# Four modulation pieces to one PSUM region, score products of two heads on opposite row halves, and two steps moved

## What is computed

```python
# both layers: six modulation vectors per stream from the conditioning
def _ada(cond, w, b):
    m = (jax.nn.silu(cond) @ w + b)[:, None, :]
    return jnp.split(m, N_MOD, axis=-1)
# even layer: scores over 128 + 64 (rotary) columns of a head, 4 heads
def _mla_block(qb, k, v):
    s = jnp.einsum('bqhd,bkhd->bhqk', qb, k).astype(jnp.float32) * MLA_SCALE
    p = jax.nn.softmax(s, axis=-1).astype(v.dtype)
    return jnp.einsum('bhqk,bkhd->bqhd', p, v)
# odd layer: 6 heads, two score maps (m) of 64 columns each
def _diff_block(qb, k, v, lam, subln_g, lam_init):
    s = jnp.einsum('bqhmd,bkhmd->bhmqk', qb, k).astype(jnp.float32) * DIFF_SCALE
    p = jax.nn.softmax(s, axis=-1)
    a = (p[:, :, 0] - lam * p[:, :, 1]).astype(v.dtype)
    o = jnp.einsum('bhqk,bkhe->bqhe', a, v)
    return _rms_norm(o, subln_g) * (1.0 - lam_init)
```

## Time and profile before

| what | value |
|---|---|
| median of 3 runs | 1722.41 us (1716.16 to 1723.5) |
| profiled execution | 1721.32 us, its span 1719.8 us |
| PE busy | 1657.8 us (96%) |
| DVE, ACT busy | 1062.3 us (62%), 942.7 us (55%) |
| DMA | 426.29 MB, mean 248 GB/s |
| chain that ended last | PE 91%, DVE 3%, ACT 3%, DMA 2% |

### The profile page before, as it was taken

How to read it: one execution, slowest core, us unless ns; L and a number is a source line. 1 busy time by engine, 2 the same in 40 slices (tenths; PEclk the granted TensorE clock), 3 DMA queues, 4 the chain that set the end, 5 groups by cost and what they waited for, 6 DMA issues and landing times.

```text
span 1719.8 us, 23106 instructions
## 1 busy us (share of the span) xinstructions
PE 1657.8 (96%) x8546; PEld 1323.3 (77%) x8546; DVE 1062.3 (62%) x1380; ACT 942.7 (55%) x1372; POOL 37.8 (2%) x60
## 2 busy tenths in 40 slices
PE   6998999899999999999988999999999999999997
PEld 3785458798888888688756888888888888888885
DVE  2341331452222333454474899999999989999998
ACT  4412432462222322462365677777877777777875
POOL 0000000040000000000000100000000000000000
PEclk9998999899999999999999999999999999999999
DMA  8524374369222222272205899999999999999992
GB/s 336 199 74 196 139 255 171 115 245 375 98 98 98 98 99 98 74 254 105 74 1 196 355 421 375 396 358 396 356 412 354 400 382 377 384 367 393 364 354 75
DMA packets 67709, 426.29 MB, mean 248 GB/s; under 512 B 8624, under 2 KB 12464, under 8 KB 19760
## 3 DMA queue, kind: packets, MB, share of 16 engines
q1 hardware_dynamic: 59856, 396.93, 60.2%
q0 software_dynamic: 7776, 28.32, 4.2%
HBM read 401.62 MB, written 23.59 MB: 247 GB/s over the span
## 4 chain that ended last, share of the span: by engine, by line
PE 91%; DVE 3%; ACT 3%; DMA 2%; issue 1%; SPq 0%; ACTq 0%; DVEq 0%
PE ps L1654 26%; PE ps L1656 26%; PE ps L1655 26%; PE ps L1672 3%; PE ps L1696 2%; PE ps L1813 2%; DMA raw<-in_w 1%; PE ps L1705 1%; PE ps L2097 1%; DMA x<-in_x 1%; PE ps L1862 1%; DVE small L1207 1%; PE ps L1844 1%; PE ps L1860 1%; DVE wl L1004 1%
## 5 line engine op out<-in xcount | busy, mean ns | idle before, releaser
L1501 DVE TENSOR_TENSOR wl<-raw,wh 128x1024 fp32r<-128x1024 f32 x522 | 615.7, 1222 | 62.4 <-ACT wh L908 55.8
L908 ACT ACTIVATE wh<-raw 128x1024 fp32r<-128x1024 f32 x522 | 523.0, 1053 | 97.1 <-PE ps L1656 97.1
L1654 PE MATMUL ps<-wh,ah 128*128 128x512 f32 (+1 forms) x800 | 310.2, 388 | 0.9 <-issue 0.2
L1654 PE MATMUL ps<-ah,wh 128*128 128x512 f32 (+1 forms) x848 | 301.9, 356 | 6.0 <-DVE al L1119 3.3
L1656 PE MATMUL ps<-wh,al 128*128 128x512 f32 (+1 forms) x800 | 302.5, 378 | 0.0
L1655 PE MATMUL ps<-wl,ah 128*128 128x512 f32 (+1 forms) x800 | 302.1, 378 | 0.0
L1655 PE MATMUL ps<-al,wh 128*128 128x512 f32 (+1 forms) x848 | 294.0, 347 | 0.0
L1656 PE MATMUL ps<-ah,wl 128*128 128x512 f32 (+1 forms) x848 | 293.9, 347 | 0.0
L1004 DVE TENSOR_TENSOR wl<-raw,wh 128x1024 fp32r<-128x1024 f32 x120 | 141.5, 1222 | 142.9 <-ACT wh L485 142.9
L1654 PEld LDWEIGHTS ps<-ah,wh 128*128 128x128 f32 x848 | 161.7, 191 | 29.7 <-issue 4.3
L1655 PEld LDWEIGHTS ps<-al,wh 128*128 128x128 f32 x848 | 161.7, 191 | 20.7 <-issue 1.0
(11 more groups left out here) (251 smaller groups left out, 1582.5 us busy)
## 6 DMA issues: line engine op xcount, KB each, us to landing
raw<-in_w SPq DMA_DIRECT2D x372, 1024.0 KB, 6.3
sent<-raw POOLq DMA_DIRECT2D x16, 512.0 KB, 24.4
back<-raw POOLq DMA_DIRECT2D x16, 512.0 KB, 25.1
x<-sent POOLq DMA_DIRECT2D x7, 512.0 KB, 12.2
back<-x POOLq DMA_DIRECT2D x7, 512.0 KB, 9.0
x<-in_x SPq DMA_DIRECT2D x1, 2048.0 KB, 13.6
raw<-in_ukv SPq DMA_DIRECT2D x1, 1024.0 KB, 7.3
out<-raw SPq DMA_DIRECT2D x4, 256.0 KB, 3.4
```

The costliest lines, as they stand in the source:

```text
L908: act.activation(wh[:, J % SPLITS, piece_half(h)], slot(J % SLOTS)[:, piece_half(h)], ACT.Copy).then_inc(w_hi, 1)
L1501: ins = dve.tensor_tensor(wl[:, J % SPLITS, piece_half(h)], slot(J % SLOTS)[:, piece_half(h)], wh[:, J % SPLITS, piece_half(h)].bitcast(F3 ...
L1654: pe.matmul(out, lh, rh, start=start, stop=False)
```

## The change

Four modulation pieces n = 4q + j now add into one region (`JOINT = 4`): piece j uses a window of `condP` that is shifted by 2j columns, so that its two data rows come to rows 2j and 2j + 1. One copy `rows(q)` and one `mod_cols(q)` (8 columns wide) serve four pieces. The pieces are spread otherwise: 8 to 11 before the projections, 12 to 30 in the even attention loop, 31 to 34 after units 2 to 5 of the even output projection, the rest as before; the ring's order follows. `take_modulation` reads the new column order. In the even attention the units of two heads alternate, and PE issues two units' scores in every other turn: both 128-row products, then both rotary products. In the odd attention the queries are evacuated with the factor -1/8, so that the minimum over the scores is the bias and L1208 goes; scaling takes two operations; the first unit's scores are issued in the middle of the last input piece, and those of unit i + 1 behind the transposes of unit i - 2. `eps` and `pick_rows` move within `small`.

```diff
+JOINT = 4
...
-NORM_MODS, ATT_MODS, GAP_MODS = 16, 35, 40
+NORM_MODS, ATT_MODS, OUT_MODS, GAP_MODS = 12, 31, 35, 40
...
-            + mods(NORM_MODS, ATT_MODS) + main(M_WOUT + 3, M_GU + 2) + mods(ATT_MODS, GAP_MODS) + main(M_GU + 2, M_OIN + 2)
+            + mods(NORM_MODS, ATT_MODS) + main(M_WOUT + 3, M_GU) + mods(ATT_MODS, ATT_MODS + 2) + main(M_GU, M_GU + 1)
+            + mods(ATT_MODS + 2, OUT_MODS) + main(M_GU + 1, M_GU + 2) + mods(OUT_MODS, GAP_MODS) + main(M_GU + 2, M_OIN + 2)
...
+        condP = area(15616, 2 * (JOINT - 1) + KD * 32)
+
+        def cond_columns(k, j):
+
+            at = 2 * (JOINT - 1) + 32 * k - 2 * j
+            return condP[:, at:at + 32]
...
-            def rows(n):
-                act.wait_ge(mod_used, n + 1)
-                if n >= 2:
-                    act.wait_ge(sem("mod_cols"), n - 1)
-                act.activation(mod_row(n), ps[:, 6 + n % 2, 0:256], ACT.Copy).then_inc(sem("mod_rows"), 1)
-            rows(0)
-            rows(1)
+            def rows(q):
+                act.wait_ge(mod_used, JOINT * q + JOINT)
+                if q >= 2:
+                    act.wait_ge(sem("mod_cols"), q - 1)
+                act.activation(mod_row(q), ps[:, 6 + q % 2, 0:256], ACT.Copy).then_inc(sem("mod_rows"), 1)
...
+                    if i == 0 and begun:
+                        begun()
...
-                    if name == "mla":
-                        rows(NORM_MODS + i)
+                    if name == "mla" and (NORM_MODS + i) % JOINT == JOINT - 1:
+                        rows((NORM_MODS + i) // JOINT)
...
-                    act.activation(q_o[:, 2 * p:2 * p + 2, :], ps[:, bank:bank + 2, 0:TL], ACT.Copy).then_inc(evac_act, 1)
+                    act.activation(q_o[:, 2 * p:2 * p + 2, :], ps[:, bank:bank + 2, 0:TL], ACT.Copy, scale=-DIFF_SCALE).then_inc(evac_act, 1)
...
+            def last_piece():
+                project(OIN - 1)
+                act.wait_ge(sem("four_ps"), 2)
+                act.activation(ah[:, 6:8, 0:TL], ps[:, 6, :].rearrange("p (a b) -> p a b", a=2), ACT.Copy
+                               ).then_inc(sem("four_hi"), 1)
...
+                            src = ps[:, 2 * ((i + 1) % 2):2 * ((i + 1) % 2) + 2, :]
+                        if name == "diff":
+                            dve.tensor_reduce(small[:, cols], src, AX.X, ALU.min).then_inc(s_("negmax"), 1)
+                        else:
+                            link(dve.tensor_reduce(small[:, cols], src, AX.X, ALU.max))
+                            dve.tensor_scalar(small[:, cols], small[:, cols], -scale, None, ALU.mult).then_inc(s_("negmax"), 1)
...
-                link(dve.tensor_scalar(small[:, at + 1:at + 2], small[:, at + 1:at + 2], small[:, 7:8], None, ALU.mult))
-                link(dve.tensor_scalar(pr_o[:, i % 2, 0, :], pr_o[:, i % 2, 0, :], small[:, at:at + 1], None, ALU.mult))
-                return dve.scalar_tensor_tensor(out=pr_o[:, i % 2, 0, :], in0=pr_o[:, i % 2, 1, :],
-                                                scalar=small[:, at + 1:at + 2], in1=pr_o[:, i % 2, 0, :],
-                                                op0=ALU.mult, op1=ALU.add)
-
-            attention("diff", ounits, DIFF_SCALE, scaled_o, lambda u: None)
+                first, second = (pr_o[:, i % 2, m, :] for m in range(2))
+                link(dve.tensor_scalar(second, second, small[:, at + 1:at + 2], small[:, 7:8], ALU.mult, ALU.mult))
+                return dve.scalar_tensor_tensor(out=first, in0=first, scalar=small[:, at:at + 1], in1=second, op0=ALU.mult, op1=ALU.add)
...
+                q, j = divmod(n, JOINT)
                 pe.wait_ge(*ring_landed("mod", n))
-                if n >= 2:
-                    pe.wait_ge(sem("mod_rows"), n - 1)
+                if j == 0 and q >= 2:
+                    pe.wait_ge(sem("mod_rows"), q - 1)
                 w = slot(ring_slot("mod", n))
                 for k in range(KD):
-                    j = 32 * (k % 4)
-                    mm = pe.matmul(ps[j:j + 32, 6 + n % 2, 0:256], condP[:, k, :], w[:, k * 256:(k + 1) * 256],
-                                   start=(k < 4), stop=(k >= 4))
+                    at = 32 * (k % 4)
+                    mm = pe.matmul(ps[at:at + 32, 6 + q % 2, 0:256], cond_columns(k, j), w[:, k * 256:(k + 1) * 256],
+                                   start=(j == 0 and k < 4), stop=(j == JOINT - 1 and k >= 4))
                 mm.then_inc(mod_used, 1)
 
-            def mod_cols(n):
-                pe.wait_ge(sem("mod_rows"), n + 1)
+            def mod_cols(q):
+                pe.wait_ge(sem("mod_rows"), q + 1)
+                at = 256 + 48 * (JOINT * q // MOD_LAYER0) + 4 * JOINT * (q % (MOD_LAYER0 // JOINT) // 2)
+                out = ps[:, 6 + q % 2, at:at + 4 * JOINT].rearrange("p (j c s) -> p j c s", c=2, s=2)
                 for c in range(2):
-                    at = 256 + 48 * (n // MOD_LAYER0) + 4 * (n % MOD_LAYER0 // 2) + 2 * c
-                    mm = pe.matmul(ps[:, 6 + n % 2, at:at + 2], mod_row(n)[:, c * P:(c + 1) * P], pick_rows,
-                                   start=True, stop=True)
+                    mm = pe.matmul(out[:, :, c, :], mod_row(q)[:, c * P:(c + 1) * P], pick_rows, start=True, stop=True)
...
             def filler(n):
 
                 mod_piece(n)
-                mod_cols(n - 1)
+                if n % JOINT == 1 and n > JOINT:
+                    mod_cols(n // JOINT - 1)
 
...
+                if n == 1:
+                    mod_cols(2)
...
+                def score(i):
+                    if paired and i % 2:
+                        return
+                    if i >= 2:
+                        pe.wait_ge(s_("exp"), i if paired else i - 1)
+                    if paired:
+                        scores(i)
+                    else:
+                        scores(i).then_inc(s_("scores"), 1)
+
                 for i in range(len(units) + 3):
-                    if i < len(units):
-                        if i >= 2:
-                            pe.wait_ge(s_("exp"), i - 1)
-                        scores(i).then_inc(s_("scores"), 1)
+                    if begun <= i < (2 + ahead if ahead else len(units)):
+                        score(i)
                     filler(i)
                     if 2 <= i <= len(units) + 1:
                         u = i - 2
@@ -1834,6 +1854,8 @@
                         for b in range(units[u][2] // P):
                             mm = pe.transpose(ps[:, tb + u % 2, b * P:(b + 1) * P], pr(u, b), ident)
                         mm.then_inc(s_("turned"), 1)
+                    if ahead and 2 <= i < len(units) - ahead:
+                        score(i + ahead)
...
             def unit_filler(i):
                 mod_piece(NORM_MODS + i)
-                if i:
-                    mod_cols(NORM_MODS + i - 1)
+                if i > 1 and (NORM_MODS + i) % JOINT == 1:
+                    mod_cols((NORM_MODS + i) // JOINT - 1)
             def scores_e(i):
-                h, j, n, k0 = units[i]
-                pe.matmul(ps[:, i % 2, 0:n], q_nope[:, h, j * P:(j + 1) * P], k_nope[:, h, k0:k0 + n], start=True, stop=False)
-                r = slice(64 * (h % 2), 64 * (h % 2) + 64)
-                return pe.matmul(ps[:, i % 2, 0:n], q_pe[r, h // 2, j * P:(j + 1) * P], k_pe[r, k0:k0 + n],
-                                 start=False, stop=True)
+                for u in (i, i + 1):
+                    h, j, n, k0 = units[u]
+                    pe.matmul(ps[:, u % 2, 0:n], q_nope[:, h, j * P:(j + 1) * P], k_nope[:, h, k0:k0 + n], start=True, stop=False)
+                for u in (i, i + 1):
+                    h, j, n, k0 = units[u]
+                    r = slice(64 * (h % 2), 64 * (h % 2) + 64)
+                    pe.matmul(ps[:, u % 2, 0:n], q_pe[r, h // 2, j * P:(j + 1) * P], k_pe[r, k0:k0 + n],
+                              start=False, stop=True).then_inc(sem("mla_scores"), 1)
             attention("mla", units, scores_e,
...
+                if u == 2:
+                    pe.wait_ge(scales_ready, 2)
+                    mod_piece(ATT_MODS)
+                if 3 <= u <= 5:
+                    filler(ATT_MODS + u - 2)
...
+            def first_scores():
+                pe.wait_ge(evac_act, evacs(("i", 8), "act"))
+                pe.wait_ge(sem("orope_done"), 4)
+                scores_o(0).then_inc(sem("diff_scores"), 1)
+
...
-    return [(h, j, T if j < 2 else TL, 0 if j < 2 else TL) for h in range(HEADS) for j in range(4)]
+    return [(h, j, T if j < 2 else TL, 0 if j < 2 else TL) for g in range(HEADS // 2) for j in range(4) for h in (2 * g, 2 * g + 1)]
```

More of the change, by code:

```diff
@@ L558, in _ @@
             root(N_E1)
-            for n in range(MOD_FIRST - 2, MOD_FIRST):
-                rows(n)
+            rows(1)
             act.wait_ge(scales_ready, 1)
@@ L586, in _ @@
             root(N_KV)
[L587 to L588 removed]
+            rows(2)
             dsts = ([q_nope[:, h, :] for h in range(HEADS)] + [q_pe[:, g, :] for g in range(HEADS // 2)]
```

146 lines of the change are left out of this document (68 added, 78 removed).

## The result

| | before | changed |
|---|---|---|
| median, us | 1722.86 (1716.16 to 1723.5, 4 runs) | 1692.51 (1691.86 to 1693.49, 4 runs) |
| profiled execution, us (span) | 1721.3 (1719.8) | 1691.86 (1690.2) |

The ratio is 0.9833, 95% interval 0.9808 to 0.9858: faster by 1.7%, clear of noise. A second series of the changed kernel gave 0.9829 (0.9815 to 0.9842), median 1691.24. The forecast was 1693.

A forecast was written before the change was run, and what follows sets the result against it. PE was taken to bound the even attention, PE and DVE to be equally busy in the odd. Terms -0.5 - 16.5 - 8.9 + 2.8 - 1.4 - 4.1 = -28.6 us from 1721.3 gave 1692.7, said as 1693; range 1683 to 1704.

The forecast's parts named there:

- before and in the projections: Projections start 14.3 us earlier, high clock saves 2.7 us, one column product adds 0.46 us: -16.5 us, bounds -18 and -10.
- even attention: Even attention: column products -6.9, paired scores -7.3, new waits +5.6, last column product gone but DVE's last subtraction awaited -0.3: -8.9 us.
- even output projection: Four pieces and one column product come in, +4.5 us; after the wait for piece 37, -1.7 us: +2.8, bounds +1 and +4.5.
- odd input projection: 712 to 770.7 us: six column products go, three behind waits, so three counted: -1.4 us, bounds 0 and -2.8.
- odd attention: DVE's unit shortens from 2.97 to 2.64 us, -3.6 us; with first maximum and scores -4.1 us in all, bounds -1.5 and -6.
- The pair: Even attention scores, two heads together: 2.87 us against 4.00, 1.6 against 2.3 with 256 keys, rotary products overlapping: -7.3 us.
- A: Low clock stays in the projections or comes earlier: gain there 2.7 to 7 us less, 1698 us; chance 0.12.
- B: Even attention: row halves don't overlap inside a bank that 128-row products opened: +6.7 us, 1699 us; chance 0.06.
- F: Column sharing fails because a region must wait for its copy: at most 1 us a region, 1700 us; chance 0.02.
- C: Waits in the even attention of 10 us or more, DVE and ACT working in bursts: 1698 us; chance 0.08.
- D: Few new waits and more gain from the later stages: 1686 us; chance 0.09.
- E: Slower than before: clock falls in the even attention, +50 us at half rate, 1743 us; chance 0.03.

The follow-up runs named there:

- Experiment 4: Changed kernel with eight modulation pieces before the projections and none in the even output projection, regions still shared by four: 1700.75 us, ratio 0.9881.
- experiment 3: Unpaired: changed kernel with one unit's scores a turn, each waiting for the exponential two turns back: 1693.61 us, ratio 0.9841.
- experiments 1: Rotary products apart: changed kernel with each head's rotary product right behind its own 128-row product: 1699.95 us, ratio 0.988.
- Experiment 7: Changed kernel with the ring filled in another order, pieces 31 to 34 and then 35, 36 before the gate/up pieces that would block them: 1689.82 us, ratio 0.9822.
- Experiment 5: Changed kernel with DVE's odd-attention turn long again, one more 2-column operation and scaling in three operations: 1697.44 us, ratio 0.9885.
- experiment 6: Changed kernel with the odd attention's scores issued late as before, ACT's last piece and DVE's low part in front: 1694.33 us, ratio 0.9855.
- 9: Changed kernel with DVE's subtraction behind the scaling of the turn instead of in front of it: 1691.4 us, ratio 0.9835.
- experiment 2: Changed kernel with both rotary products of a pair on rows 0 to 63, order and waits unchanged: 1697.91 us, ratio 0.9867.

## Why the prediction was right, point by point

| step | forecast, us | measured, us |
|---|---|---|
| start | -0.5 | -1.3 |
| before and in the projections | -16.5 | -16.7 |
| even attention | -8.9 | -8.1 |
| even output projection | +2.8 | +4.0 |
| odd input projection | -1.4 | -3.9 |
| odd attention | -4.1 | -4.7 |
| rest | 0 | +1.1 |
| sum, spans | -28.6 | -29.6 |

The odd attention is counted with the +1.3 us by which the stretch in front of it grew, mostly the first scores' 1.1 us: -5.95 + 1.3. The rest is the odd output projection with the router, 56.6 and 57.5 us, and the experts. That the sums agree to 1 us is in part luck: the seven differences add up to 7.2 us without their signs.

- **Before the projections.** The projections began 14.4 us earlier counted from the first large matmul (forecast 14.3), and at the high clock: no low clock between 43.2 and 315.7 us. Experiment 4 brings both back, though it prices the whole move at 8 to 9.5 us net of the output projection where the forecast's terms make 12 (16.5 less 4.5); the part with which shared regions speed up eight pieces, 3.1 us (24.2 to 21.1), had no term of its own.
- **Even attention.** The column products were sized right (-6.9 against -6.6 of busy time, experiment 3). The pair was priced too high (-7.3 against -5.3) and the waits as well (+5.6 against +3.2); these two errors cancel to 0.3 us, which is luck. Most of the remaining error is the last term, forecast at -0.3: from before to unpaired the idle time rose by 0.5 us (0.64 to 1.18). In the pair's term the overlap is full, as the earlier trace rows had it. The Trainium skill's 3.07 times for four row tiles, 77% of the full factor (TensorE: Matmul & The Clock Gate, section on packing small matmuls), would by the prediction's estimate make 1.36 us of a rotary pair; measured are 1.05. Of the 2.0 us by which the pair's term is off, the score products are 0.3: the changes of row count were mis-sized, 0.2 us and not 0.1, so that a pair of 512 keys takes 2.97 and not 2.87 us. 0.7 us is the dearer work beside modulation pieces, for which the sum had no term, and 1.0 us are waits that the profile books as work (experiment 3). The 66.82 - 63.83 = 3.0 us of busy time between unpaired and rotary products apart, which hold the same instructions, divide in the same way: 1.3 us in the 128-row scores (a unit behind value products takes 2.0 us, one behind other scores 2.11), 1.3 in the value products, 0.4 in the rest.
- **Even output projection.** Pieces and products came to what was forecast, but "nothing in the change frees it sooner, so that wait and the dip of the clock behind it stay" missed that the ring's order also puts pieces 35 and 36 behind the second gate/up piece, which waits for the first one's split. PE's waits for transfers went from 3.3 to 5.2 us. Experiment 7 takes 3.1 of them away: -3.6 us.
- **Odd input projection.** The step that failed most, outside its own bounds: "three stand behind waits for normalised chunks, so I count three". All six column products came off PE's busy time (53.85 to 50.63 us). The waits did not grow in their place: idle time fell by 0.7 us as well, a wait of 0.9 us for a transfer among it.
- **Odd attention.** The turn is 2.58 us, not 2.64. Experiment 5 shows DVE's operations, 0.39 us a turn in ten turns. Of the early scores experiment 6 shows +1.8 us, but most of it is their place behind the transposes, which the prediction gave no term, and 0.4 us the first maximum off the path. The stage before and after had some low clock each (0.94 and 0.96), so its -4.7 us are good to about 1 us only.
- **Rivals.** A, B and F didn't occur. C and D stayed out: 4.4 us idle in the attention, between them. E didn't occur in the changed kernel (even attention at 1.00 in both profiles), but showed for a few microseconds in experiments 4 and 9. The prediction's "the transfers hold" is so in both profiles of the changed kernel, but not in those of all variants: PE waited for transfers in the loop 0.3 us in experiments 1 and 2, 1.7 in 4, 2.1 in 5 and 2.5 in 9.

## What to carry to other kernels

When two small-row matmuls can sit on opposite row halves, put them next to each other: the overlap was whole, and the saved changes of row count were worth another half of it (as much again at 256 columns). But count what the burst does to its neighbours: of 7.0 us saved in the score products some 0.7 went back because other products got dearer next to modulation pieces, and some 4.2 because the next engines came late. Against single units the pair gave 2.0 us, too little for the totals to show. When a step moves in a ring with few slots, write down for every later transfer which use frees its slot and what stands in front of it in the queue, and look whether a large operand nobody needs yet holds it up.

## What the runs showed of the hardware that was not expected

- A change between 128-row and 64-row instructions costs 0.2 us each way (a 512-key pair of eight instructions 4.22 us with three changes inside, 3.82 with one). It isn't the row count alone: 128-row scores behind a modulation piece of 32 columns pay it too, four instructions in 1.91 us (190.64 to 192.55 in experiment 2) where four steps of 0.43 make 1.72.
- A weight load is hidden behind a running matmul on the same 64 rows (0.18 us in a step of 0.22, experiment 2); two matmuls on opposite halves run at the same time.
- The place of the low clock moves between executions of one program: in the odd attention, clock 0.96 and 0.93 in two profiles of the changed kernel, 45.15 and 45.96 us, and 43.53 us at 1.00 with the same attention code. Terms of 1 to 2 us in such a stage can't be read from one profile.
